# High and low part of the activation in one product of 512 columns, with VectorE adding the halves

## The reference, cut to what matters

```
# second layer's MLP of the first block (l = 1), w1: 1024 x 4096, w2: 4096 x 1024
sq_relu_mlp(h, w1, w2) = square(relu(h @ w1)) @ w2
# second block, after rmsnorm: the first four parts of the projection
proj = h @ w_in            # rq, rk, ..., mq, mk: queries and keys of two branches
# second block, expert retrieval
q = (ht @ w_q).reshape(T, PEER_HEADS, 2, half)     # w_q: 1024 x 2048
```

## Time and profile before

| | |
|---|---|
| median of the runs | 1881.33 us |
| profiled execution, its own time | 1885.04 us |
| its span, first to last instruction | 1883.1 us |
| TensorE busy | 1822.7 us (97%) |
| VectorE, ScalarE, POOL busy | 66%, 46%, 53% |
| mean granted TensorE clock | 0.99 |

### The profile page before, as it was taken

The page is one execution under the profiler, slowest core; times in us unless marked ns, Lnnn a source line. Parts: engine busy times, 40 slices in busy tenths (PEclk is TensorE's granted clock), DMA queues, the critical chain, the costliest instruction groups (busy, mean ns, idle before and its releaser), DMA issues.

```text
span 1883.1 us, 32518 instructions
## 1 busy us (share of the span) xinstructions
PE 1822.7 (97%) x11582; PEld 1591.2 (84%) x11582; DVE 1246.9 (66%) x2546; ACT 869.0 (46%) x1407; POOL 998.2 (53%) x431
## 2 busy tenths in 40 slices
PE   5999899999999999999999999999999999999999
PEld 2747579987979997988878899999999998888887
DVE  6586667878556446132233179899999957777776
ACT  3033555445445545542453556634444445545544
POOL 4043146443765443764447778866666654444443
PEclk8999999999999999999999999999999999999999
DMA  8786247886655554643324555544444455555555
GB/s 321 261 310 241 78 145 244 279 264 208 207 195 188 183 187 144 202 145 105 109 91 156 168 178 180 179 146 146 146 146 146 146 179 194 194 192 191 196 192 167
DMA packets 95328, 346.09 MB, mean 184 GB/s; under 512 B 10544, under 2 KB 12032, under 8 KB 94592
## 3 DMA queue, kind: packets, MB, share of 16 engines
q1 hardware_dynamic: 78048, 283.67, 45.2%
q10 hardware_dynamic: 17184, 61.11, 9.3%
HBM read 343.66 MB, written 1.08 MB: 183 GB/s over the span
## 4 chain that ended last, share of the span: by engine, by line
PE 77%; DVE 15%; DMA 4%; ACT 2%; POOL 1%; issue 1%; ACTq 0%; DVEq 0%; SPq 0%
PE ps L532 30%; PE ps L581 28%; DMA ring<-stream 2%; PE ps L737 2%; PE ps L516 2%; PE ps L804 2%; PE ps L651 2%; PE ps L751 2%; DVE hot_hi_a L2642 2%; DVE hot_lo_a L2643 1%; DVE hot_lo_b L2643 1%; DVE hot_hi_b L2642 1%; PE ps L967 1%; POOL ring_lo L477 1%; DVE arena L2653 1%
## 5 line engine op out<-in xcount | busy, mean ns | idle before, releaser
L477 POOL TENSOR_TENSOR ring_lo<-ring,ring_hi 128x1024 fp32r<-128x1024 f32 x371 | 897.5, 2423 | 703.3 <-ACT ring_hi L471 701.9
L471 ACT ACTIVATE ring_hi<-ring 128x1024 fp32r<-128x1024 f32 x502 | 531.0, 1059 | 462.1 <-DMA ring<-stream 458.2
L532 PE MATMUL ps<-h_lo,ring_hi 128*128 128x256 f32 x2096 | 295.3, 284 | 0.0
L532 PEld LDWEIGHTS ps<-h_lo,ring_hi 128*128 128x128 f32 x2096 | 271.5, 193 | 0.0
L581 PE MATMUL ps<-ring_hi,e_pair 128*128 128x512 f32 x1024 | 253.7, 389 | 0.9 <-DVE e_pair L2677 0.9
L2677 DVE TENSOR_TENSOR e_pair<-arena,e_pair 128x256 fp32r<-128x256 f32 x128 | 174.5, 1363 | 99.0 <-ACT e_pair L1751 98.8
L581 PEld LDWEIGHTS ps<-ring_hi,e_pair 128*128 128x128 f32 x1024 | 192.1, 188 | 41.0 <-issue 1.3
L477 DVE TENSOR_TENSOR ring_lo<-ring,ring_hi 128x1024 fp32r<-128x1024 f32 x141 | 178.0, 1263 | 39.2 <-ACT ring_hi L471 38.9
L581 PE MATMUL ps<-ring_hi,arena_r 128*128 128x512 f32 x672 | 174.5, 392 | 0.5 <-ACT ring_hi L471 0.5
L532 PE MATMUL ps<-late_r,ring_hi 128*128 128x256 f32 x1136 | 162.7, 286 | 0.4 <-ACT arena L1304 0.4
L532 PE MATMUL ps<-late_r,ring_lo 128*128 128x256 f32 x1136 | 159.5, 283 | 0.0
(11 more groups left out here) (304 smaller groups left out, 2515.2 us busy)
## 6 DMA issues: line engine op xcount, KB each, us to landing
ring<-stream SPq DMA_DIRECT2D x540, 512.0 KB, 3.3
arena<-aside_w ACTq DMA_DIRECT2D x49, 512.0 KB, 4.7
late<-aside_w ACTq DMA_DIRECT2D x21, 512.0 KB, 4.5
resid<-aside_w ACTq DMA_DIRECT2D x10, 512.0 KB, 6.2
arena<-scale_w ACTq DMA_DIRECT2D x8, 512.0 KB, 16.0
arena<-ln_rows ACTq DMA_DIRECT2D x8, 512.0 KB, 5.0
arena<-gate_cols ACTq DMA_DIRECT2D x2, 1024.0 KB, 5.1
arena<-decay ACTq DMA_DIRECT2D x1, 1536.0 KB, 6.9
```

Source lines behind the costliest of these rows:

```text
L471: act.activation(ring_hi[:, s, :], ring[:, s, :], ACT.Copy).then_inc(hi_ready, 1)
L477: eng.tensor_tensor(ring_lo[:, s, :], ring[:, s, :], ring_hi[:, s, :], ALU.subtract).then_inc(lo_ready[s], 1)
L532: m = pe.matmul(ps[:, bank, 0:T], w[:, kc * P:(kc + 1) * P], x[:, kc, :], start=begin, stop=w is w_lo and kc == KC - 1)
```

## The change

In 28 of the 32 up tiles of the second MLP and in 14 of the 16 tiles of each query stage, `h_tile` gives way to `h_pair_tile`: w_hi meets x_hi and x_lo in one product of 512 columns, whose halves go to the two halves of the bank, and w_lo with x_hi adds to the first half. VectorE then adds the halves with a reduction (`sum_of_halves`) that writes the tile to SBUF and frees the bank; ScalarE no longer reads these banks. In the MLP, ScalarE's Relu now works from SBUF, after VectorE's sum. VectorE makes the sum of tile j+1 ahead of its work on hidden tile j.

```diff
+            def h_pair_tile(u, parts, h_hi, bank, i=None):
+                w_hi, w_lo = split_unit(u, i)
+                start_fill(bank)
+                for kc in range(KC):
+                    m = pe.matmul(ps[:, bank, :], w_hi[:, kc * P:(kc + 1) * P], parts[kc], start=kc == 0, stop=False,
+                                  skip_group_check=True)
+                    if kc == 0:
+                        m.then_inc(units_begun, 1)
+                wait_unit_lo(u, i)
+                for kc in range(KC):
+                    m = pe.matmul(ps[:, bank, 0:T], w_lo[:, kc * P:(kc + 1) * P], h_hi[:, kc, :], start=False,
+                                  stop=kc == KC - 1, skip_group_check=True)
                 m.then_inc(full[bank], 1)
                 fills[bank].add()
...
                 def down_up(j, i=None):
                     wait_hi, wait_lo = hid_waits()
                     rows_unit(u0 + 4 + 2 * j, hid_hi[:, j % 4, :], hid_lo[:, j % 4, :], wait_hi, wait_lo, i, first=j == 0)
-                    h_tile(u0 + 5 + 2 * j, h_hi_1, 4 + j % 2, i)
+                    if l == 0:
+                        h_tile(u0 + 5 + 2 * j, h_hi_1, 4 + j % 2, i)
+                    else:
+                        h_pair_tile(u0 + 5 + 2 * j, h_parts_1, h_hi_1, 4 + j % 2, i)
...
-            h_tiles("in2_qk", 16, h_hi_2)
+            h_tiles("in2_qk", 16, h_hi_2, h_parts_2)
...
-            h_tiles("peer_q", 16, h_hi_3)
+            h_tiles("peer_q", 16, h_hi_3, h_parts_3)
...
+                def summed_hidden(j):
+                    b = 4 + j % 2
+                    act.wait_ge(emptied[b], drains[b].add())
+                    act.activation(hid[:, j % 4, :], hid[:, j % 4, :], ACT.Relu).then_inc(relu_done, 1)
+                    act.wait_ge(relu_done, n_relu.add())
+                    act.activation(hid2[:, j % 4, :], hid[:, j % 4, :], ACT.Square).then_inc(hid_ready, 1)
...
+                with rolled(act, 6, [(drains[4], 2), (drains[5], 2), (n_relu, 4)]) as i:
+                    for j in range(7, 11):
+                        summed_hidden(j)
                         unit_hi(act, u0 + 2 * j, i)
                         unit_hi(act, u0 + 2 * j + 1, i)
...
-            with rolled(act, 2, [(drains[4], 4), (drains[5], 4)]) as i:
-                for n in range(8):
-                    split_and_drain("in2_qk", n, zz[:, i * 8 + n, :], i=i)
+            for n in range(2):
+                split_and_drain("in2_qk", n, zz[:, n, :])
+            for n in range(2, 16):
+                unit_hi(act, FIRST_UNIT["in2_qk"] + n + 2)
+                drains[4 + n % 2].add()
+            act.wait_ge(emptied[4], drains[4].now())
             act.wait_ge(emptied[5], drains[5].now())
...
+            def sum_of_halves(dst, b, fill, i=None, per=0):
+                dve.wait_ge(full[b], at_trip(i, per, fill))
+                dve.tensor_reduce(dst, ps[:, b, :].rearrange("p (a t) -> p t a", a=2), AX_X, ALU.add).then_inc(emptied[b], 1)
+
+            def summed_tiles(stage, dst, n_tiles):
+                first = mark["first", stage]
+                for n in range(2, n_tiles):
+                    sum_of_halves(dst[:, n, :], 4 + n % 2, first[n % 2] + n // 2)
...
-                with rolled(dve, 7, [(n_hid, 4)]) as i:
-                    for j in range(3, 7):
+                hidden(3)
+                unit_lo(dve, u0 + 6)
+                up_sum(4)
+                for j in range(4, 7):
+                    up_sum(j + 1)
+                    hidden(j)
+                    unit_lo(dve, u0 + 2 * j)
+                with rolled(dve, 6, [(n_hid, 4)]) as i:
+                    for j in range(7, 11):
+                        up_sum(j + 1, i)
                         hidden(j)
                         unit_lo(dve, u0 + 2 * j, i)
                 hidden(31)
...
             rms_norm(block1_x, "mix_g", h_hi_2, second_row)
+            summed_tiles("in2_qk", zz, 16)
...
             rms_norm(block2_x, "ffn_g", h_hi_3)
+            summed_tiles("peer_q", qp, 16)
```

More of the change, by code:

```diff
@@ L247, in build, with h_part @@
         late_r = rounded("late_r", "late", [P, 2048])
-        h_lo = rounded("h_lo", "h", [P, KC, T])
+        h_span = rounded("h_span", "arena", [P, (at["h"] - at["arena"]) // 4 + KC * T])
+        def h_part(like, skip=0):
+            first = (at[like] - at["arena"]) // 4 + skip
+            return h_span[:, first:first + KC * T].rearrange("p (a b) -> p a b", a=KC)
+        h_lo = h_part("h")
         gate_r = rounded("gate_r", "gate_lo", [P, T])
@@ L284, in build, with h_parts @@
         rstd = area(30720, 2, 512)
-        h_hi_1 = arena_r[:, 10752:12800].rearrange("p (a b) -> p a b", a=KC)
-        h_hi_2 = arena_r[:, 19456:21504].rearrange("p (a b) -> p a b", a=KC)
-        h_hi_3 = late_r[:, :].rearrange("p (a b) -> p a b", a=KC)
+        h_hi_1, h_hi_2, h_hi_3 = h_part("arena", 10752), h_part("arena", 19456), h_part("late")
+        def h_parts(like, skip):
+            first = (at[like] - at["arena"]) // 4 + skip
+            apart = (at["h"] - at["arena"]) // 4 - first
+            views = []
+            for kc in range(KC):
+                a = h_span[:, first + kc * T:first + (kc + 1) * T]
+                views.append(bass.AP(a.tensor, a.offset, [a.ap[0], [apart, 2], [1, T]]))
+            return views
+        h_parts_1, h_parts_2, h_parts_3 = h_parts("arena", 10752), h_parts("arena", 19456), h_parts("late", 0)
         hid_hi = arena_r[:, 12800:13824].rearrange("p (a b) -> p a b", a=4)
@@ L441, in build @@
         hid_ready = sem("hid_ready")
+        relu_done = sem("relu_done")
         hid_hi_ready = sem("hid_hi_ready")
@@ L535, in h_tile @@
                             m.then_inc(units_begun, 1)
+                m.then_inc(full[bank], 1)
+                fills[bank].add()
+            def h_pair_tile(u, parts, h_hi, bank, i=None):
[7 more added lines that the diff above has]
+                wait_unit_lo(u, i)
+                for kc in range(KC):
+                    m = pe.matmul(ps[:, bank, 0:T], w_lo[:, kc * P:(kc + 1) * P], h_hi[:, kc, :], start=False,
+                                  stop=kc == KC - 1, skip_group_check=True)
                 m.then_inc(full[bank], 1)
@@ L1006, in down_up @@
                     rows_unit(u0 + 4 + 2 * j, hid_hi[:, j % 4, :], hid_lo[:, j % 4, :], wait_hi, wait_lo, i, first=j == 0)
-                    h_tile(u0 + 5 + 2 * j, h_hi_1, 4 + j % 2, i)
+                    if l == 0:
+                        h_tile(u0 + 5 + 2 * j, h_hi_1, 4 + j % 2, i)
+                    else:
+                        h_pair_tile(u0 + 5 + 2 * j, h_parts_1, h_hi_1, 4 + j % 2, i)
                 first_tiles(u0, h_hi_1)
+                mark["up", l] = (fills[4].n, fills[5].n)
                 for j in range(2, 4):
@@ L1021, in mlp, with h_tiles @@
                            [w[0] for w in waits], [w[1] for w in waits])
-            def h_tiles(stage, n_tiles, h_hi):
+            def h_tiles(stage, n_tiles, h_hi, parts=None):
                 u = FIRST_UNIT[stage]
                 first_tiles(u, h_hi)
+                mark["first", stage] = (fills[4].n, fills[5].n)
                 for n in range(2, n_tiles):
-                    h_tile(u + n, h_hi, 4 + n % 2)
+                    if parts is None:
+                        h_tile(u + n, h_hi, 4 + n % 2)
+                    else:
+                        h_pair_tile(u + n, parts, h_hi, 4 + n % 2)
             turn_rows()
@@ L1607, in mlp @@
                     return
+                n_relu = Count()
+                def summed_hidden(j):
[4 more added lines that the diff above has]
+                    act.activation(hid2[:, j % 4, :], hid[:, j % 4, :], ACT.Square).then_inc(hid_ready, 1)
                 for j in range(3):
@@ L1610, in mlp @@
                     unit_hi(act, u0 + 3 + j)
-                with rolled(act, 7, [(drains[4], 2), (drains[5], 2)]) as i:
-                    for j in range(3, 7):
-                        hidden(j)
+                hidden(3)
+                unit_hi(act, u0 + 6)
+                unit_hi(act, u0 + 7)
+                for j in range(4, 7):
+                    summed_hidden(j)
+                    unit_hi(act, u0 + 2 * j)
+                    unit_hi(act, u0 + 2 * j + 1)
+                with rolled(act, 6, [(drains[4], 2), (drains[5], 2), (n_relu, 4)]) as i:
+                    for j in range(7, 11):
+                        summed_hidden(j)
                         unit_hi(act, u0 + 2 * j, i)
                         unit_hi(act, u0 + 2 * j + 1, i)
-                hidden(31)
+                summed_hidden(31)
                 unit_hi(act, u0 + 62)
@@ L1730, in _ @@
             norm_to_h(param("ffn_g", 0, 8), None, h_hi_3, FIRST_UNIT["peer_q"], rms=True)
[L1731 to L1735, removed]
+            for n in range(2):
+                split_and_drain("peer_q", n, qp[:, n, :])
+            for n in range(2, 16):
+                if n < 14:
+                    unit_hi(act, FIRST_UNIT["peer_q"] + n + 2)
```

(6 more changed lines are left out.)

## The result

The changed kernel takes 1916.45 us (median of 4 runs, 1910.40 to 1919.62), the kernel before beside it 1881.14 us: ratio 1.0166, 95% interval 1.0144 to 1.0188, so 27 to 35 us slower, 31 by the ratio itself. The profiled execution took 1919.62 us with a span of 1917.7, which is 34.6 us more than that of before.

A forecast was written before the change was run, and what follows sets the result against it. TensorE, busy 97% of the span, was taken as the bound. Second MLP +32.0, branch stage -1.1 and expert queries -0.6 make +30.3 us on the median of 1881.33: 1911.5 us, range 1898 to 1930.

The forecast's parts named there:

- The likeliest case: Whole kernel: TensorE waits each second-MLP period for VectorE's low part behind the sum; 1911.5 us, chance 0.73.
- Rival A: Second MLP: nothing waits and only the products count, -3.9 us to 1877.4 us; chance 0.10.
- The products: Changed tiles: fewer products save 0.08 us a tile, 2.79 for 2.87 us; 2.2 us in the second MLP.
- The sum of halves: VectorE's reduction in all changed tiles: 0.69 us each, between 0.42 and 1.0 us.
- Rival B: Second MLP: POOL holds VectorE's cast every period, or the sum costs 1.0 us; 1920 to 1926 us, chance 0.14.
- The stall: Second MLP: TensorE waits 1.13 us a period for VectorE's low part, period 6.67 us, 26 times, 29.4 us.
- the last pair: VectorE's subtraction and low part in the second MLP: the low part starts 0.08 us before the subtraction's end.
- The pieces of the residual: Second MLP, units 9 to 19: POOL's residual work holds VectorE's subtraction in about every other period, 4 us in all.
- Rival C: Second MLP: idle stretches drop TensorE's granted clock to half in one period of four; 1942 us, chance 0.03.
- The end: Second MLP's last group: TensorE has less done when the last unit arrives, +0.8 us.
- The query stages: Branch and expert queries: sums hidden, tiles shorter; -1.1 us in the branch stage, -0.6 us in the expert queries.
- three tiles' saving: Expert queries: what tiles 2 to 4 save is lost waiting for POOL's low part, leaving 11 tiles, 0.9 us.

The follow-up runs named there:

- e1: The changed kernel with VectorE's sum of tile j+1 moved behind hidden j and the low part of unit 2j; 0.9969 of the kernel before.
- e6: The changed kernel with VectorE's order low part of unit 2j, sum of tile j+1, hidden j; 0.9980 of the kernel before.
- e7: The kernel before with only the second MLP changed, the sum behind hidden j and the low part; 0.9981 of the kernel before.
- e5: The changed kernel with POOL making the residual's eight pieces ahead of unit 5's low part in the second MLP; 1.0151 of the kernel before.
- e3: The kernel before with only the two query stages changed; 0.9995 of the kernel before.
- e2: The changed kernel with both query stages' tiles as before, only the second MLP changed; median 1918.04 us, 1.0161 of the kernel before.
- e4: The changed kernel with each sum of halves in the second MLP made twice, one after the other; median 1930.42 us, 1.0242 of the kernel before.

## Why the prediction was right

**Direction and place.** The likeliest case came: 1911.5 us forecast, 1916.45 measured, or +31 us by the ratio for the +30.3 of the sum. TensorE's wait for L494 on VectorE shows 27 times, and moving one instruction (e1, e6) takes it away. Rival A is out.

**The products.** 2.79 us a tile in the branch stage, as counted from the earlier trace rows. In the MLP the 28 periods of e1, e6 and e7, which have no stall, last 154.37 us for 157.36 before: 3.0 us gained for 2.2. The stage as a whole gains only 1.7 (e1) to 2.7 us (e6), because its last group or the norm behind it is longer.

**The sum of halves.** 0.691 us for 0.69; never longer, beside POOL or not (that at 588.92 lies wholly beside POOL's low part of 588.45 to 590.85). Rival B's dearer sum is out.

**The stall.** Period 6.57 us for 6.67. Most of the difference is an overlap that I had given only to the last pair: the cast, too, starts 0.08 us before the sum's record ends. And POOL's low part was over before the cast, as worked out, so the casts between 640 and 765 us have a median of 283 ns. Over 26 periods +0.95 each: 24.7 us, where 26 x 1.05 = 27.3 stood.

**The pieces of the residual.** The mis-sized term. The tiles' ends from 588.90 to 635.48 make six periods of 46.6 us; at 6.57 each they were 39.4. So 7.2 us instead of 4. Of these, 2.9 are the clock, which the term left out: at 593.6 the products up to the next w_lo take 2.08 + 2.28 us for 1.20 + 1.82, and at 623.4 it is 1.73 + 2.89, which makes 1.3 + 1.6 us. The other 4.3 are POOL's, near the 4 that were counted, though not in the way that was counted. The subtraction is held only in the first of the six periods, on top of a held cast. Later it is the cast that ends just after the piece, with 1.22, 0.47 and 1.33 us at 606.15, 613.63 and 620.38, and the subtraction takes 0.42 each time. Rival C thus happened in two periods, here behind the two longest stalls, and not through the whole stage. e5 takes both out and its stage falls by 6.4 us.

**The end.** From the last tile's end to the norm's next VectorE work 10.9 us for 10.3, +0.6 for the +0.8 counted. With 0.35 us in the norm, which no term had, the sum is 24.7 + 7.2 + 0.6 + 0.35 - 0.2 (two periods without a stall) = 32.65, beside 32.6 measured. That the forecast of 32.0 lies so near is partly luck: 2.6 us too much for the stalls and 3.2 too little for the pieces cancel.

**The query stages.** The branch stage's 14 tiles took 39.12 us for 40.32, so -1.2 for -1.1. In the expert queries it was 42.08 us for 43.79 from the last 16 products of the two first tiles to the products behind the last tile, so -1.7 for the -0.6 counted. The step that didn't hold is that TensorE would lose three tiles' saving to POOL's low part: in the changed kernel's trace it waits for nothing there, while in e3's it does, 0.31 us. And ScalarE's drains, put at nothing, held TensorE up in the trace before. This one stood behind a high part that had waited 3.96 us for its transfer.

```profile
1058.42 1.19 PE L532 MATMUL ps<-late_r,ring_hi 128*128 128x256 f32 x8 [0.36 <-ACT arena L1304]
```

In e2 and e7, which drain with ScalarE too, that wait is absent and the stretch takes 42.99 us, so the change itself is worth 0.9 us there. The total of e3 can't tell -1.7 from nothing.

The version that beats both kernels is e1, at 0.9969 of the kernel before.

## What to carry to other kernels

When an engine gets an instruction that waits for the bound engine's newest result, look at what stands behind it in its queue: if the bound engine needs that next, what the chain takes beyond the bound engine's own work up to that point (eight products here) is added to every period, however idle the engine is on average. Here VectorE's share was 66% before and after, and moving one line from ahead of two others to behind them turned 31 us lost into 4 to 6 us gained (e6, e1). A product of twice the columns saves only the overhead of a product, 0.01 us each here, so such a change has little to pay a wait with.

## What the runs showed of the hardware that I had not expected

- The reduction of 128x512 to 128x256 from PSUM, reading in steps of 256 elements, costs the same 0.69 us as one of 128x512 to 128x1.
- In the changed kernel one stall of 2.88 us was followed by a granted clock of 0.79 over 594 to 600, one of 1.79 us by 0.73 over 624 to 630; regular stalls of 0.74 and even 1.47 us (e4) in every period left it at 1.00. In e2 a stall of 2.76 us left it at 1.00 too, and one of 1.81 us was followed by 0.82. So the length of the stall alone doesn't decide.
- A held cast costs only where TensorE waits behind it. In the second MLP the cast takes 1.15 to 1.82 us in e1 (median 1.22) and 0.30 us in the median of e7, whose MLP has the same code, and the 28 periods last 154.37 us in both. In the changed kernel the cast of 1.47 us is part of the stall of 2.88 us.
